# First stage of a hybrid layer kernel: modulation in row form, recurrence state loaded early, four store slots, norms one tile later

## What is computed

```python
def modulation(cond, w_ada, b_ada):
    m = jax.nn.silu(cond) @ w_ada + b_ada            # 1024 -> 6 * 1024, for two conditions
    return jnp.split(m[:, None, :], 6, axis=-1)

def mixer_inputs(h, p):                              # h = x * (1 + scale1) + shift1
    z = h @ p['w_in']
    za, zq, zk, zv, zu, zg = split_cols(z, [A_COLS, D_MIX, D_MIX, D_MIX, D_MIX, 3 * D_MODEL])
    return token_shift_mix(za, p['rwkv_mu']), zq, zk, zv, zu, zg

def rwkv_prep(za, p):
    r, k, v, lw, la, lg = split_cols(za, [D_MIX, D_MIX, D_MIX, 2 * A_LORA_W, 2 * A_LORA_A, A_LORA_G])
    w = p['rwkv_w0'] + einsum('btnr,nrc->btnc', tanh(lw), p['rwkv_w2'])
    a = sigmoid(p['rwkv_a0'] + einsum('btnr,nrc->btnc', la, p['rwkv_a2']))
    kk = (k * p['rwkv_kk']).reshape(bsz, t, A_HEADS, A_HD)
    kk = kk / maximum(norm(kk, axis=-1), 1e-12)
    k_dir = k * (1 + (a - 1) * p['rwkv_ka'])
    ...
```

## Time and profile before

| | |
|---|---|
| median of 3 runs | 2528.96 us (2528.1 to 2529.77) |
| the profiled execution's own time | 2519.51 us |
| span of its instructions | 2517.7 us |
| TensorE busy with matmuls | 2066.8 us, 82% of the span |
| VectorE, ScalarE, GpSimd busy | 933.0, 491.8, 685.4 us |
| the first stage | from 0 to about 546 us |

### The profile page before, as it was taken

One profiled execution on the slowest core, in us unless ns is written; L12 is line 12 of the kernel. 1 busy time (PEld: TensorE's weight loads), 2 busy tenths in 40 slices (PEclk: granted clock), 3 DMA queues, 4 the chain that ended last, 5 costly groups with the idle time before them and its releaser, 6 DMA issues. The chain is left out here.

```text
span 2517.7 us, 41126 instructions
## 1 busy us (share of the span) xinstructions
PE 2066.8 (82%) x16339; PEld 1575.7 (63%) x16339; DVE 933.0 (37%) x1863; ACT 491.8 (20%) x928; POOL 685.4 (27%) x1030
## 2 busy tenths in 40 slices
PE   7989879979769989999999975975829999999800
PEld 7666545546548777777777765932528888877600
DVE  0734221207624444333454332734251222222267
ACT  0211122112123233232332312100102222212100
POOL 4416000000013233232332211312013444444423
PEclk9989878789989898888998887997769999999955
DMA  7233344545131120211210016600128998999572
GB/s 236 67 117 101 122 138 139 175 173 191 59 115 52 44 73 19 59 57 34 66 40 24 7 49 246 214 33 18 45 73 323 334 322 305 334 341 323 211 308 100
DMA packets 244753, 358.31 MB, mean 142 GB/s; under 512 B 38305, under 2 KB 173236, under 8 KB 240772
## 3 DMA queue, kind: packets, MB, share of 16 engines
q1 hardware_dynamic: 216734, 299.42, 35.2%
q0 software_dynamic: 24560, 45.27, 5.0%
q10 hardware_dynamic: 3318, 11.59, 1.3%
HBM read 308.42 MB, written 85.65 MB: 157 GB/s over the span
## 5 line engine op out<-in xcount | busy, mean ns | idle before, releaser
L440 PE MATMUL ps_s<-hT,w_in_sb 128*128 128x512 f32 x432 | 214.6, 654 | 0.0
L2688 DVE TENSOR_TENSOR me_hh<-me_sg,ps_ju 128x128 f32<-128x128 f32 x76 | 21.9, 288 | 398.8 <-PE ps_jd L2645 375.3
L1262 PE MATMUL ps_gs<-hT,gt_w 128*128 128x512 f32 x256 | 147.6, 660 | 11.0 <-PEq L75 7.3
L440 PEld LDWEIGHTS ps_s<-hT,w_in_sb 128*128 128x128 f32 x432 | 89.9, 214 | 105.1 <-issue 104.9
L2637 PE MATMUL ps_jg<-me_xT,me_wg 128*128 128x128 f32 x1216 | 149.0, 276 | 0.0
L2637 PE MATMUL ps_ju<-me_xT,me_wu 128*128 128x128 f32 x1216 | 148.2, 275 | 0.0
L2645 PE MATMUL ps_jd<-me_wd,me_hh 128*128 128x512 f32 x304 | 143.9, 596 | 2.4 <-DVE me_yb L2694 2.4
L2637 PEld LDWEIGHTS ps_jg<-me_xT,me_wg 128*128 128x128 f32 x1216 | 142.7, 193 | 0.1
L2637 PEld LDWEIGHTS ps_ju<-me_xT,me_wu 128*128 128x128 f32 x1216 | 141.9, 192 | 0.0
L2666 ACT ACTIVATE me_xT<-ps_jx 128x1024 f32<-128x1024 f32 x77 | 78.9, 1024 | 256.7 <-PE ps_jx L2628 256.7
L2628 PEld LDWEIGHTS ps_jx<-ident,me_xg 128*128 128x128 f32 x616 | 79.4, 192 | 72.2 <-DMA me_xg<-h_dram,me_ids 43.1
(11 more groups left out here) (536 smaller groups left out, 4207.3 us busy)
## 6 DMA issues: line engine op xcount, KB each, us to landing
me_wg<-in_exp_w_gate SPq DMA_DIRECT2D x76, 512.0 KB
me_wu<-in_exp_w_up SPq DMA_DIRECT2D x76, 512.0 KB
me_wd<-in_exp_w_down SPq DMA_DIRECT2D x76, 512.0 KB
cb_rows<-yj_dram SPq DMA_DIRECT2D x10, 2048.0 KB
w_ad_sb<-in_w_ada SPq DMA_DIRECT2D x32, 512.0 KB
w_in_sb<-in_w_in SPq DMA_DIRECT2D x31, 512.0 KB
gt_w<-in_w_in SPq DMA_DIRECT2D x24, 512.0 KB, 4.1
zr<-in_w_ada SPq DMA_DIRECT2D x4, 2048.0 KB, 10.6
```

What stands on the lines that cost most here:

```text
L440: mm(ps_s[:, b, :], w_in[:, r, k, :], hT[:, k, 0:TS], start=(k == 0), stop=(k == KT - 1))
L1262: nc.tensor.matmul(ps_s[:], w[:, t % WR, k, :], hT[:, k, 0:TS], start=(k == 0), stop=(k == KT - 1))
```

## The change

1. **First modulation in row form.** The two columns of silu(c) become the stationary operand, and a block's 512 columns are streamed: 8 products per block into `ps_s[0:2]`. ScalarE copies the 2x512 result into `adr` (in `zst`), TensorE turns it in four pieces into the same places of `ps_ad`. Block j's turns come behind the products of block j+1. On ScalarE the copies of blocks 1 to 3 stand ahead of the exponentials and sines for the S5 powers.
2. **Recurrence state.** `s_in` gets a buffer of its own, and SyncE loads it at the head, behind the fourth tile of `w_in`, instead of in round 17.
3. **Four store slots** for turned tables: piece n waits for the store of piece n-4.
4. **Norms** go from tiles 18, 19 to 19, 20; the low-rank products start in tile 21 instead of 20, with 3, 3, 3, 3, 2, 2 per tile.
5. The turn of the new keys waits also for VectorE's half of the eviction.

```diff
-NORM_TAU = {18: (0, 1), 19: (2, 3)}
-LORA_TAU = {20: (0, 1, 2), 21: (3, 4, 5), 22: (6, 7), 23: (8, 9), 24: (10, 11), 25: (12, 13), 26: (14, 15)}
+NORM_TAU = {19: (0, 1), 20: (2, 3)}
+LORA_TAU = {21: (0, 1, 2), 22: (3, 4, 5), 23: (6, 7, 8), 24: (9, 10, 11), 25: (12, 13), 26: (14, 15)}
...
-        at_st = xs[:, G_N * P:G_N * P + 2 * 512].rearrange("p (b n) -> p b n", b=2)
+        at_more = s5b("s5_atx", [P, 2, 512])
+        at_st = [xs[:, G_N * P + b * 512:G_N * P + (b + 1) * 512] for b in range(2)] + [at_more[:, b] for b in range(2)]
...
                     if j >= 2:
-                        sp.wait_ge(m.s_ada, 4 * (j - 1))
+                        sp.wait_ge(m.s_ada, j - 1)
...
+                sp.dma_start(s_in[:], a["state_rwkv"].rearrange("d h v k -> v d h k")).then_inc(m.r_st, 16)
...
-                        sp.dma_start(s_in[:], a["state_rwkv"].rearrange("d h v k -> v d h k")).then_inc(m.r_st, 16)
...
+                def ada_rows(j):
+                    pe.wait_ge(land_b[j % 2], 16 * (j // 2 + 1))
+                    if j >= 2:
+                        pe.wait_ge(m.s_adr, j - 1)
                     for k in range(KT):
-                        last = mm(ps_ad[:, 2 * i:2 * i + 2], w_ada[:, j % 2, k, c * P:(c + 1) * P], m.c_silu[:, k, :],
-                                  start=(k == 0), stop=(k == KT - 1))
+                        last = mm(ps_s[0:2, j % 2, :], m.c_silu[:, k, :], w_ada[:, j % 2, k, :], start=(k == 0), stop=(k == KT - 1))
                     last.then_inc(m.s_ada, 1)
...
+                def ada_turn(j):
+                    pe.wait_ge(m.s_adr, j + 1)
+                    for c in range(4):
+                        i = 4 * j + c
+                        last = turn(ps_ad[:, 2 * i:2 * i + 2], adr[:, j % 2, c * P:(c + 1) * P], m.ident[0:2, 0:2])
+                    last.then_inc(m.s_adt, 1)
+                ada_rows(0)
+                for j in range(1, 4):
+                    ada_rows(j)
+                    if j == 1:
                         pe.wait_ge(m.s_p5, 64)
                         turn(px[1][:, 0:P], rows[:], m.ident[:]).then_inc(m.s_p5_mm, 1)
+                    ada_turn(j - 1)
+                ada_turn(3)
...
+                        pe.wait_ge(m.s_z_dve, tau)
...
+                def ada_evict(j):
+                    act.wait_ge(m.s_ada, j + 1)
+                    if j >= 2:
+                        act.wait_ge(m.s_adt, j - 1)
+                    A(adr[:, j % 2], ps_s[0:2, j % 2, :], ACT.Identity).then_inc(m.s_adr, 1)
+                ada_evict(0)
                 act.wait_ge(m.s_d5, 16)
...
+                for j in range(1, 4):
+                    ada_evict(j)
                 act.wait_ge(m.s_sin, 1)
...
-                    if n >= 2:
-                        act.wait_ge(at_out[n % 2], 16 * (n // 2))
+                    if n >= 4:
+                        act.wait_ge(at_out[n % 4], 16 * (n // 4))
...
-                dve.wait_ge(m.s_ada, 16)
+                dve.wait_ge(m.s_adt, 4)
```

More of the change, by code:

```diff
@@ L161, in front_phase @@
         px = [pb(f"ps_x{i}", [P, 512]) for i in range(3)]
+        s_in = sb("rw_sin", [HD, 2, HEADS, HD])
         s5c = ctx.enter_context(ExitStack())
@@ L186, in front_phase @@
         w2, a2 = sb("rw_w2", [P, MIX]), sb("rw_a2", [P, MIX])
-        s_in = sb("rw_sin", [HD, 2, HEADS, HD])
         sg, bds = sb("rw_sg", [P, 4, N]), sb("rw_bd", [P, 2, N])
@@ L192, in front_phase @@
         kp_sb = sb("kp_sb", [P, MIX])
+        adr = zst[0:2, :, 0:512]
         cm, cmT = sb("ad_cm", [P, 64]), sb("ad_cmT", [64, P])
@@ L198, in front_phase @@
          m.s_z_out1, m.s_pad, m.s_mu, m.s_nb, m.s_zs, m.s_sh, m.s_kp_mm, m.s_kp, m.s_kp_out, m.s_v_mm, m.s_v_sb, m.s_v_out0,
-         m.s_v_out1, m.s_nv_out, m.s_cm, m.s_cm_mm, m.s_cmT, m.s_cm_out) = sems(
+         m.s_v_out1, m.s_nv_out, m.s_cm, m.s_cm_mm, m.s_cmT, m.s_cm_out, m.s_adr, m.s_adt) = sems(
             nc, m, "s_c s_x s_b0 s_b1 s_w0 s_w1 s_w2 s_w3 s_a0 s_a1 s_ident s_pcol_mm s_pcol s_silu s_ada s_mod s_xt_mm s_ht "
             "s_z_mm s_z_act s_z_dve s_ad_mm s_z_out0 s_z_out1 s_pad s_mu s_nb s_zs s_sh s_kp_mm s_kp s_kp_out s_v_mm "
-            "s_v_sb s_v_out0 s_v_out1 s_nv_out s_cm s_cm_mm s_cmT s_cm_out")
+            "s_v_sb s_v_out0 s_v_out1 s_nv_out s_cm s_cm_mm s_cmT s_cm_out s_adr s_adt")
         (m.s_p5, m.s_p5c, m.s_d5, m.s_p5b, m.s_p5_mm, m.s_c5_mm, m.s_pc, m.s_csb, m.s_dt, m.s_sin, m.s_exps, m.s_dve5,
-         m.s_pl5, m.s_bb, m.s_msk0, m.s_msk, m.s_vt, m.s_at, m.s_at_mm, m.s_at_sb, m.s_at_o0, m.s_at_o1, m.s_t_mm, m.s_tm,
+         m.s_pl5, m.s_bb, m.s_msk0, m.s_msk, m.s_vt, m.s_at, m.s_at_mm, m.s_at_sb, m.s_at_o0, m.s_at_o1, m.s_at_o2, m.s_at_o3, m.s_t_mm, m.s_tm,
          m.s_t_sb, m.s_vt_out, m.s_tt_out) = sems(
             nc, m, "s_p5 s_p5c s_d5 s_p5b s_p5_mm s_c5_mm s_pc s_csb s_dt s_sin s_exps s_dve5 s_pl5 s_bb s_msk0 s_msk s_vt "
-            "s_at s_at_mm s_at_sb s_at_o0 s_at_o1 s_t_mm s_tm s_t_sb s_vt_out s_tt_out")
+            "s_at s_at_mm s_at_sb s_at_o0 s_at_o1 s_at_o2 s_at_o3 s_t_mm s_tm s_t_sb s_vt_out s_tt_out")
         (m.r_w, m.r_st, m.r_pool, m.r_blk, m.r_lev, m.r_st_mm, m.r_sm, m.r_act, m.r_kk, m.r_sq, m.r_n_mm, m.r_rt, m.r_dve,
@@ L213, in front_phase @@
         land_b, land_w, land_a = [m.s_b0, m.s_b1], [m.s_w0, m.s_w1, m.s_w2, m.s_w3], [m.s_a0, m.s_a1]
-        z_out, v_out, at_out = [m.s_z_out0, m.s_z_out1], [m.s_v_out0, m.s_v_out1], [m.s_at_o0, m.s_at_o1]
+        z_out, v_out, at_out = [m.s_z_out0, m.s_z_out1], [m.s_v_out0, m.s_v_out1], [m.s_at_o0, m.s_at_o1, m.s_at_o2, m.s_at_o3]
         vt_out, sg_out, bd_out = [m.r_v_o0, m.r_v_o1], [m.r_o0, m.r_o1, m.r_o2, m.r_o3], [m.r_bo0, m.r_bo1]
@@ L232, in overlay_free @@
             eng.wait_ge(m.s_vt_out, 64)
-            for n in range(2):
-                eng.wait_ge(at_out[n], 16 * 8)
+            for n in range(4):
+                eng.wait_ge(at_out[n], 16 * 4)
         def last_z_out(tau):
@@ L288, in _ @@
                             sp.wait_ge(m.s_at_sb, n + 1)
-                            sp.dma_start(m.at_dram[c, d, :, 512 * j4:512 * j4 + 512], at_st[:, n % 2]).then_inc(at_out[n % 2], 16)
+                            sp.dma_start(m.at_dram[c, d, :, 512 * j4:512 * j4 + 512], at_st[n % 4]).then_inc(at_out[n % 4], 16)
                     if tau == 5 or tau == 13:
@@ L297, in _ @@
                         sp.dma_start(m.tt_dram, tt.rearrange("p g q -> p (g q)")).then_inc(m.s_tt_out, 16)
-                        for n in range(2):
-                            sp.wait_ge(at_out[n], 16 * 8)
+                        for n in range(4):
+                            sp.wait_ge(at_out[n], 16 * 4)
                         sp.wait_ge(m.s_vt_out, 64)
@@ L502, in _ @@
                 pe.wait_ge(m.s_silu, 1)
[L503 to L506, removed]
+                def ada_rows(j):
+                    pe.wait_ge(land_b[j % 2], 16 * (j // 2 + 1))
+                    if j >= 2:
+                        pe.wait_ge(m.s_adr, j - 1)
                     for k in range(KT):
-                        last = mm(ps_ad[:, 2 * i:2 * i + 2], w_ada[:, j % 2, k, c * P:(c + 1) * P], m.c_silu[:, k, :],
-                                  start=(k == 0), stop=(k == KT - 1))
+                        last = mm(ps_s[0:2, j % 2, :], m.c_silu[:, k, :], w_ada[:, j % 2, k, :], start=(k == 0), stop=(k == KT - 1))
                     last.then_inc(m.s_ada, 1)
-                    if i == 7:
+                def ada_turn(j):
[8 more added lines that the diff above has]
+                    if j == 1:
                         pe.wait_ge(m.s_p5, 64)
                         turn(px[1][:, 0:P], rows[:], m.ident[:]).then_inc(m.s_p5_mm, 1)
+                    ada_turn(j - 1)
+                ada_turn(3)
                 pe.wait_ge(m.s_x, 16 * NT)
@@ L618, in at_evict @@
                     act.wait_ge(m.s_at_mm, n + 1)
-                    if n >= 2:
-                        act.wait_ge(at_out[n % 2], 16 * (n // 2))
+                    if n >= 4:
+                        act.wait_ge(at_out[n % 4], 16 * (n // 4))
                     if n == 0:
                         act.wait_ge(m.s_xt_mm, KT)
-                    A(at_st[:, n % 2], px[2][:], ACT.Identity).then_inc(m.s_at_sb, 1)
+                    A(at_st[n % 4], px[2][:], ACT.Identity).then_inc(m.s_at_sb, 1)
                 def squared(f):
```

## The result

| | before | changed |
|---|---|---|
| median with the first timing, 4 runs each | 2528.53 us | 2448.28 us |
| ratio, 95% interval | | 0.9692 (0.967 to 0.9714) |
| second timing, medians of 17 and 5 runs | 2525.14 us | 2445.97 us |
| ratio, 95% interval | | 0.968 (0.9665 to 0.9695) |
| profiled execution's own time | 2519.51 us | 2447.38 us |

About 79 us were saved where 67.6 were forecast, and the time lies 4 us under the range. That it would be faster was right and most steps of the sum were close, but the total was too small.

What follows compares the result with a forecast made beforehand. TensorE, working nearly without pause, was taken to bound the first stage, with eviction and state-load waits and clock falls to win back. Savings of 40.6 + 14 + 13.0 = 67.6 us took 2528.96 to 2461.4 us; range 2452 to 2481.

Steps and rivals of the forecast that it cites:

- four slots (tiles 6 to 9, 14 to 17): Table-piece eviction waits go: tiles 6 to 9 save 19.7 us, 14 to 16 19.0, tile 17 1.9; sum 40.6.
- head, up to tile 0: Row form at full clock after a 3.2 us start-up: first eviction at 57.0 instead of 70.55; 14 us saved.
- from the end of tile 17 to the value tiles: 169.6 us becomes 156.6: the state's wait goes, nearly 8 us return in low-rank products; 13.0 saved.
- the price of a fall of the clock: Tiles 6 to 9: each eviction wait costs about 3.2 us beyond its idle, as products behind it run slower.
- Rival (e): Table pieces: the wait for slots is one for ScalarE itself; 40.6 us stay, 27 saved, 2502 us; chance 0.02.
- Rival (a): Head: row form at the lower clock throughout, 14.2 us a block; 49.2 us saved, 2479.8 us; chance 0.20.
- The neighbour that I took: Products at 666 to 670 us, 80 stationary and 128 streamed columns, clock 1.00; taken as guide for the row form.
- the sum's term for tiles 25 and 26: Last two low-rank tiles: 33.3 us, as the five tiles from 415.54 to 498.89 take 16.7 each.
- From the profiled execution to the median: Whole kernel: the same 67.6 us saved for both, 2519.5 to 2451.9 us profiled and 2528.96 to 2461.4 us median.
- (b): Waits for sg slots spread: tiles 23 and 24 also get a late store, 4 to 6 us each; 2472 us; chance 0.08.
- (d): Four sg slots become the bound: seven sigmoids wait for stores, 2543 us at 12 us each; chance 0.03.
- Rival (c): Low-rank tiles wait less or the clock doesn't fall in them; 8 us gained, 2453 us; chance 0.05.

Runs made afterwards that it cites:

- slots_only: The kernel before with four store slots alone; 2485.96 us, ratio 0.9853 to the kernel before.
- kk_behind: The changed kernel with SyncE's round 22 issuing the low-rank products' stores ahead of those of kk and lgs; 2447.6 us, ratio 0.9708 to the kernel before.
- kk_zv: kk_behind with the value tiles' stores issued between the last loads of w_ada instead of behind them; 2444.88 us, ratio 0.9665 to the kernel before.
- after_oldplan: The changed kernel with the old tile numbers for norms and low-rank products; 2463.07 us, ratio 0.9763 to the kernel before.
- shift1: The changed kernel with one more 512-column product, its result thrown away, ahead of tile 20; first stage ends at 473.2 us, no whole time given.
- vt_between: The changed kernel with the four value turns of tiles 21 to 25 right behind the first low-rank product; 2449.17 us, ratio 0.9699 to the kernel before.

## Why the prediction was right and wrong, step by step

| term | forecast | in the traces |
|---|---|---|
| four slots (tiles 6 to 9, 14 to 17) | 40.6 | 40.7 |
| head, up to tile 0 | 14 | 16.1 |
| from the end of tile 17 to the value tiles | 13.0 | 17.3 |
| value tiles | 0 | -1.9 |
| first stage | 67.6 | 72.2 |
| between the medians | 67.6 | 79 |

**The slots** were right to 0.1 us in this pair of traces. That close it is luck, as these seven tiles before vary by 3 us between the four executions (129.2 to 132.3). Right with them is the price of a fall of the clock as part of each wait: 9.5 us of tiles 6 to 9 were not idle and went all the same. Rival (e) is out by slots_only.

**The head** was right in mechanism, and each step was a little shorter than I had it. The first eviction came at 54.95 instead of 57.0, and the 2.0 us between are made of a landing of block 1 0.4 us earlier, its products 0.5 shorter (9.84 for 10.3), turns 0.4 shorter, block 3 without the 0.6 us of waiting that I gave it (0.3 after block 2's end), the products of blocks 2 and 3 0.1, and 0.35 from block 3's end to the eviction. The turns of x ran without a low start. Rival (a), the row form at 1.2 GHz, is out: blocks 2 and 3 take 7.03 us and the clock is 1.00 there. The neighbour that I took gave the right value; that long streaming against a short weight load is the reason was not tested apart.

**The norms and the low-rank products.** The step that failed is the sum's term for tiles 25 and 26, 33.3 us, taken as two tiles with a fall of the clock like all of the five before. They took 28.0 us in the changed kernel, 5.3 less; in all its three profiled executions they kept the clock. I read a price that was the same in five tiles as a property of the tile; kk_behind and kk_zv show that it varies between executions of the same code. Tiles 23 and 24 were 0.7 us shorter than the 21.0 each. Against this stand 1.5 us for a fall in tile 18, which I had at 10.7 (12.2 measured), and 0.2 in small differences, so that 4.3 are left. Tile 22 was forecast at 24.8 and took 24.97, with 3.7 us more of waiting forecast and 5.64 - 1.58 = 4.1 measured: that the waits spread to more slots was right, and kk_behind shows the store named. The prediction had TensorE wait about 6 us if the norms stayed in tile 18; it waited 5.0 in state_only and 6.3 in after_oldplan, and moving them was worth about 5 us beside the clock of tiles 25 and 26. My later thought, that seven tiles for the low-rank products would win it back, was wrong: in after_oldplan each of tiles 22 to 26 holds two products, has no wait of TensorE, and still takes 16.0 to 16.9 us.

**The value tiles** I had left out: the store wait on ScalarE, 17.8 us before and 19.0 now, reaches TensorE by 1.3 us and one fall.

**From the profiled execution to the median.** I carried the sum over unchanged, with the remark that what is saved is the same for both. The profiled execution of before was 9 us under its median, that of after within 1 us of its own. One of three further executions had 3.9 us more in just the stage that the change shortens. With the means of the profiled executions the stage gives 75 us. This step failed too, and with 7 us it is the largest part of the 11 that were missing; with the 4.6 us of the terms above it put the time below 2452. Of its 7 us I can place 3, and 4 stay open: the later stages, whose time varied from 1970.4 to 1980.1 us and was longer in the changed kernel's profiled executions, cover them without proving anything.

Rivals (b) and (d) are out as well: tiles 23 and 24 take 20.3 and 20.9 us where 21.0 was the working's figure, and all waits for sigmoids sum to 11.0 us. The range was too narrow on its low side. Rival (c), that the clock doesn't fall in the low-rank tiles, had 0.05 and is what came in tiles 25 and 26; its 2453 lay at the edge of the range, which left no room for a second gain beside it.

## What to carry to other kernels

A wait of about 3.4 us on TensorE cost about twice what the view of waits shows (20.3 us of idle, 40.7 saved), for what followed ran at half the clock: cost a removed wait by the length of a stalled tile less that of a clean one. Where the clock falls anyway, only the wait itself comes back, as in kk_behind (4.0 us of wait, 4.0 of tile 22). When a long wait goes, look for the next one behind the same store and move its user away in the same edit: here the wait was 16.7 us, the load alone gave 7.0, and the move of the norms about 5 more. And before a sum is carried from one profiled execution to a median, ask how far that execution is from the median, and whether the part that is removed is one that varies.

## What the runs showed of the hardware

- With two stationary columns and 512 streamed ones TensorE came to 2.4 GHz within block 1 and stayed there (7.03 us for 16 records), where with 128 stationary and two streamed columns it was at 1.2 GHz for 57 us. The view of the granted clock shows 1.00 for both, in the windows from 36 and from 44 us before and from 40 to 44 us after; only the durations tell.
- The fall of the clock in tiles of low-rank products is not fixed by the code: tile 25 took 14.66 and 16.79 us in two executions of the same instructions up to there, and in shift1 and vt_between a fall moved from tile 18 to tile 19 ahead of the edit. With the old tile numbers, though, it was there in seven executions of seven.
- The 256 KB load of the state, in pieces of 256 bytes (64 values), was issued at 41.8 us, behind block 3, and landed 8.3 us later without a delay that the traces show: tile 0's piece of the modulation, whose load stands behind it, ran without a wait. In state_only, the kernel before with this load added, tile 0 began at 78.14 us, against 77.66 to 78.41 in the four executions of before.
